# Two steps of the gathered experts moved on VectorE: the last modulation sums and the additions of the dense result to x

## The reference, cut to what matters

```python
sh1, sc1, g1, sh2, sc2, g2 = jnp.split(mod, 6, axis=-1)
...
h = rms_norm(x, norm2_g[layer]) * (1.0 + sc2) + sh2
x = x + g2 * grouped_moe(h, router_w, router_b, exp_w_gate[layer],
                         exp_w_up[layer], exp_w_down[layer])
```

```python
for e in range(N_EXPERTS):
    he = jax.nn.silu(t @ w_gate[e]) * (t @ w_up[e])
    y = y + combine[:, e:e + 1] * (he @ w_down[e]).astype(jnp.float32)
```

## Time and profile before

| | |
|---|---|
| median of three runs | 2367.88 us (2359.84 to 2372.94) |
| the profiled execution's own time | 2363.46 us |
| its span | 2361.7 us |
| mean granted clock of PE | 0.986 |
| PE busy | 2254.4 us (95%) |
| DVE busy | 1470.2 us (62%) |
| ACT busy | 1081.3 us (46%) |
| gathered experts of layer 0 | about 401 to 658 us |
| gathered experts of layer 1 | about 963 to 1195 us |

### The profile page before, as it was taken

One profiled execution on the slowest core, in us unless ns is written; L12 is line 12 of the kernel. 1 busy time (PEld: TensorE's weight loads), 2 busy tenths in 40 slices (PEclk: granted clock), 3 DMA queues, 4 the chain that ended last, 5 costly groups with the idle time before them and its releaser, 6 DMA issues.

```text
span 2361.7 us, 36488 instructions
## 1 busy us (share of the span) xinstructions
PE 2254.4 (95%) x15884; PEld 1967.8 (83%) x15884; DVE 1470.2 (62%) x1411; ACT 1081.3 (46%) x1125; POOL 69.5 (3%) x128
## 2 busy tenths in 40 slices
PE   6998999989989999999999999999999999999999
PEld 4677888767787799877789999887999899878998
DVE  5766889678855655798855554555555555545454
ACT  4344334467646433577643345334333443435332
POOL 2030010000000000000000000000000000020000
PEclk9999999899999999999999999999999999999999
DMA  9854999789842264799855552004555555433553
GB/s 344 309 181 164 318 318 322 247 289 378 321 143 89 67 238 169 251 365 368 301 171 183 186 174 86 2 4 148 192 184 191 169 179 196 161 95 107 179 192 112
DMA packets 261119, 477.81 MB, mean 202 GB/s; under 512 B 8464, under 2 KB 150896, under 8 KB 257632
## 3 DMA queue, kind: packets, MB, share of 16 engines
q1 hardware_dynamic: 251264, 431.81, 52.6%
q0 software_dynamic: 9696, 43.66, 5.5%
HBM read 473.30 MB, written 2.14 MB: 201 GB/s over the span
## 4 chain that ended last, share of the span: by engine, by line
PE 78%; DVE 8%; DMA 6%; ACT 5%; issue 2%; SPq 0%; DVEq 0%; ACTq 0%
PE psum L977 7%; PE psum L979 7%; PE psum L978 7%; PE psum L994 3%; PE psum L995 3%; PE psum L996 3%; DVE w_lo L2594 3%; PE psum L948 3%; PE psum L950 3%; PE psum L949 3%; PE psum L1361 3%; PE psum L1362 3%; PE psum L1363 3%; PE psum L1276 2%; PE psum L1278 2%; PE psum L1277 2%
## 5 line engine op out<-in xcount | busy, mean ns | idle before, releaser
L2594 DVE TENSOR_TENSOR w_lo<-ring,w_hi 128x2048 fp32r<-128x2048 f32 x320 | 730.9, 2289 | 455.0 <-ACT w_hi L1987 450.7
L1987 ACT ACTIVATE w_hi<-ring 128x2048 fp32r<-128x2048 f32 x320 | 611.5, 1914 | 543.1 <-PE psum L979 140.4
L977 PE MATMUL psum<-h_hi,w_hi 128*128 128x256 f32 x1408 | 398.9, 283 | 1.6 <-DVE h_lo L3245 1.3
L979 PE MATMUL psum<-h_hi,w_lo 128*128 128x256 f32 x1408 | 398.4, 283 | 0.0
L978 PE MATMUL psum<-h_lo,w_hi 128*128 128x256 f32 x1408 | 398.4, 283 | 0.0
L977 PEld LDWEIGHTS psum<-h_hi,w_hi 128*128 128x128 f32 x1408 | 270.1, 192 | 3.6 <-issue 1.7
L978 PEld LDWEIGHTS psum<-h_lo,w_hi 128*128 128x128 f32 x1408 | 270.1, 192 | 1.4
L979 PEld LDWEIGHTS psum<-h_hi,w_lo 128*128 128x128 f32 x1408 | 270.1, 192 | 0.0
L2594 DVE TENSOR_TENSOR w_lo<-pool,w_hi 128x2048 fp32r<-128x2048 f32 x65 | 148.8, 2290 | 49.0 <-ACT w_hi L1987 48.4
L1361 PE MATMUL psum<-w_hi,h_hi 128*128 128x512 f32 x384 | 157.4, 410 | 10.3 <-DVE w_lo L2594 10.0
L1987 ACT ACTIVATE w_hi<-pool 128x2048 fp32r<-128x2048 f32 x65 | 124.6, 1917 | 69.4 <-PE psum L1363 17.0
(11 more groups left out here) (456 smaller groups left out, 3983.2 us busy)
## 6 DMA issues: line engine op xcount, KB each, us to landing
ring<-in_exp_w_down SPq DMA_DIRECT2D x48, 1024.0 KB, 7.3
ring<-in_exp_w_gate SPq DMA_DIRECT2D x47, 1024.0 KB, 7.1
ring<-in_ffn_pre_w_in SPq DMA_DIRECT2D x44, 1024.0 KB, 5.1
ring<-in_ffn_post_w_in SPq DMA_DIRECT2D x44, 1024.0 KB, 5.1
ring<-in_exp_w_up SPq DMA_DIRECT2D x32, 1024.0 KB, 6.7
pool<-in_exp_w_up SPq DMA_DIRECT2D x32, 1024.0 KB, 8.1
ring<-in_ada_w SPq DMA_DIRECT2D x24, 1024.0 KB, 7.2
pool<-in_ada_w POOLq DMA_DIRECT2D x32, 768.0 KB, 6.1
```

Of the source, the lines that this page charges most:

```text
L977: pe.matmul(o, wh[:, k, fs], h_hi[:, k, :], start=k == 0, stop=False)
L979: m = pe.matmul(o, wl[:, k, fs], h_hi[:, k, :], start=False, stop=k == KD - 1)
L1987: act.activation(w_hi[:, (s["split"] + r) % 3, :], piece(s["pieces"][r]), ACT.Copy)\
L2594: dve.tensor_tensor(w_lo[:, slot, :], piece(s["pieces"][r]), w_hi[:, slot, :].bitcast(F32), ALU.subtract).then_inc(sem("w_lo"), 1)
```

## The change

In the loop over the gathered experts, for expert 0, part 30 of the sums no longer stands between the two up pieces' low parts but at the end of the body, and part 31 moves to the end of the body of expert 1. The two additions to x no longer stand together in the body of expert 3; the first goes to the end of expert 2's body, the second to the end of expert 3's. The loads, and the orders of PE, ACT, POOL and SP, stay as they are.

```diff
@@ -2986,20 +2986,12 @@
                 for e in range(SPARSE):
                     n = at["egate", e, 0]
                     split(n + 2)
-                    if e == 0:
-                        ada_part(4 * WIDE - 2)
                     split(n + 3)
-                    if e == 0:
-                        ada_part(4 * WIDE - 1)
                     if e == 0:
                         dve.wait_ge(sem("w_used"), U0 + at["down", WIDE - 1, 0] + 1)
                         for t in range(NT):
                             m = dve.tensor_tensor(y_slots[t], bank(2 * t, 2), grow[layer][1], ALU.mult)
                         m.then_inc(sem("wide_in"), 1)
-                    if e == 3:
-                        dve.wait_ge(sem("wide_in"), layer + 1)
-                        for t in range(NT):
-                            step(dve.tensor_tensor(x[:, t, :], x[:, t, :], y_slots[t], ALU.add))
                     if layer == 0 and e == MOD_AT + 1:
                         mod_cols(1, (0, 1), 3)
                     if e == 5:
@@ -3017,6 +3009,13 @@
                                              in1=bank(5), op0=ALU.mult, op1=ALU.mult).then_inc(sem("weighted"), 1)
                     for j in range(n + 6, at["egate", e + 1, 0] + 2 if e + 1 < SPARSE else 6 * NE):
                         split(j)
+                    if e == 0:
+                        ada_part(4 * WIDE - 2)
+                    if e == 1:
+                        ada_part(4 * WIDE - 1)
+                    if e in (2, 3):
+                        dve.wait_ge(sem("wide_in"), layer + 1)
+                        step(dve.tensor_tensor(x[:, e - 2, :], x[:, e - 2, :], y_slots[e - 2], ALU.add))
                     if e == 10:
                         scattered(0)
                         scattered(1)
```

## The result

The changed kernel takes 2371.9 us (median of 20 runs, 2364.52 to 2382.31), the kernel before 2367.56 us in as many. The ratio is 1.0023, with a 95% interval of 1.0013 to 1.0033: slower by 0.23%, about 5 us, inside the range that was given, and on the side of the forecast, which was +1.4 us. Three executions among all those behind the table further down ran far longer, for a reason that is not known (2883.11 and 11943.38 us of "part 31 only", 4447.60 us of the kernel before beside "kept busy, 8"); the ratios leave them out, and without its two "part 31 only" has a median of 2371.5 us.

The account below looks back on a forecast made before the run. PE bounds the kernel from 550 us on in layer 0 and in layer 1, the supply of pieces from 475 to 500 us. Terms +2.8 + 1.8 - 2.0 - 1.2 = +1.4 us gave 2369.3 us, range 2360 to 2377.

Parts of the forecast that it names:

- Piece 4 early, 3 of the 4 us lost at piece 5: Experts 0 and 1, layer 0: PE begins piece 4 4 us earlier; piece 5's load does not move, losing 3 us.
- Part 31 too late: Ahead of layer 0's modulation: PE waits about 4.2 us for part 31; start moves +2.8 us, ends 0 and +4.8.
- The modulation at half the clock: Layer 0's 64 modulation matmuls run at half the clock after the wait, 12.9 us against 11.13: +1.8 us.
- The additions, layer 0: Expert 3, layer 0: without the additions there, piece 21's low part comes earlier, -2.0 us; ends -2.5 and 0.
- The additions, layer 1: Layer 1: PE's wait ahead of expert 2's first down matmul goes, -1.2 us; other end 0.
- Sum: Whole kernel: +2.8 + 1.8 - 2.0 - 1.2 = +1.4 us, 2369.3 us on the median.
- The rival of the early start that carries through: Layer 0: pieces 5 to 11 come faster, modulation starts at 434.4 with part 31 done; -7.7, 2360.2 us; chance 0.15.
- The rival of the additions: Layer 0: freed time goes into load waits, part 31's wait as reckoned or longer; 2372.5 to 2374.5 us; chance 0.20.
- The rivals of the clock: Half clock at pieces 4 to 9 (2374.7 us, chance 0.10), or from piece 11 to 22 (2381.9 us, chance 0.05).
- the cold start of the clock at pieces 4 to 9: Experts 0 and 1: small gaps leave PE at half clock, modulation 8.2 us late; +6.8, 2374.7 us; chance 0.10.

Follow-up runs that it names:

- part 31 only: The change, but part 30 stays between pieces 2 and 3 as before, only part 31 moved to expert 1's end; 2372.93 us, ratio 1.0020 to the kernel before.
- kept busy, 8: The change, with 8 matmuls of 256 columns on constants put on PE into the wait for part 31; 2369.34 us, ratio 1.0011 to the kernel before.
- kept busy, 13: The change, with 13 matmuls of 256 columns on constants put on PE into the wait for part 31; 2371.78 us, ratio 1.0013 to the kernel before.
- sums-only: The change, but the additions to x stand together in expert 3 as before, only the sums moved; 2373.1 us, ratio 1.0024 to the kernel before.
- part 31 early: The change, but part 31 stands right behind part 30 at expert 0's end, ahead of piece 6; 2367.24 us, ratio 0.9991 to the kernel before.
- sums in the gap: The change, but parts 30 and 31 between low parts of pieces 4 and 5: 2362.99 us, 0.9977; with modulation behind expert 2's gate pieces too: 2360.79 us, 0.9981.
- modulation later: The change, but PE does the 64 modulation matmuls behind expert 2's two gate pieces; 2360.65 us, ratio 0.9972 to the kernel before.

## Why the prediction was right, point by point

- *Piece 4 early, 3 of the 4 us lost at piece 5*: right in the waits, 0.9 and 2.5 us on PE against forecast ones of 1 and 2.4. PE began piece 4 3.4 us earlier. I had it ready for the modulation 1.5 us earlier than before (436.9 against 438.4); it was ready no earlier, 37.0 us after the first gate matmul (41.0 less the wait) against 37.1.
- *Part 31 too late*: right, in place and size. A wait of 4.0 us was measured, 4.2 forecast; part 31 began at 440.61 and ended at 442.4, 441.1 forecast. The start moved by 3.9 us where the sum had +2.8, inside the ends of 0 and +4.8. The difference is piece 9: it had its low part at 435.4 (from 433.12) and not at 434.1, after DVE had waited 2.68 us for its high part. That lateness is there from piece 5 on, whose low part was ready at 420.85 and not at 419.6; 0.3 us of it is the later first gate matmul.
- *The modulation at half the clock*: right in kind, the term that was mis-sized. I took 64 x 0.202 = 12.9 us, against the 11.1 of one execution: +1.8. The 0.202 was a misreading: the two windows of the earlier trace rows hold 26 and 42 records, 68 for 64, since one that reaches over a window's edge is counted on both sides. Counted over longer windows it is 0.111 at the full clock ("kept busy, 13": 9 records in each us from 448 to 452) and 0.216 at half. Measured with the wait unfilled: 13.8 in the change, in the sums-only and in the part-31-only run. Without the wait the length was 11.3, 8.7, 11.1, 10.3, 9.7, 9.7 in six executions of as many kernels, 10.1 on average (in two of them at the later place); what sets it is not shown. If the kernel before has this average too, and its one profile a long form, the term is 13.8 - 10.1 = +3.7 us; against its own profile it is 13.8 - 11.3 = +2.5, and not +1.8. I should have bounded it by all 64 at the full clock as well: 64 x 0.111 = 7.1 us.
- *The additions, layer 0*: -2.0 forecast, -1.7 and -3.7 measured, each in one pair of executions. Right as far as that goes.
- *The additions, layer 1*: -1.2 forecast, -1.1 measured (215.2 to 215.4 us in every kernel that moves them, 216.4 in the two that do not; PE's idle time falls from 5.1 to 3.9 us). Right.
- *Sum*: with the measured terms, +3.9 + 3.7 - 2.7 - 1.1 = +3.8 us, where the medians say +4.3 and the ratio +5.4; with +2.5 for the modulation it is +2.6. The forecast was +1.4, so it had a quarter to a third of the loss. Both positive terms were too small, and that the time lay inside the range says little, since the range was 17 us wide.
- *The rival of the early start that carries through*: it did not happen; part 31 excluded it, as argued.
- *The rival of the additions*: that the additions give nothing back (2372.5 to 2374.5 us) is nearer to the median of 2371.9 than the forecast of 2369.3; the stages speak against it, layer 1 in every kernel, layer 0 in single executions.
- *The rivals of the clock*: the cold start of the clock at pieces 4 to 9 (whose matmuls would end at 445.6, not 445.8, by its own sum) did not show in the profile of the change: the clock stayed at 1.00 from 414 to 423.7 us, over gaps of 0.9 and 2.5 us (first row below). But it was nearer than I thought. In both "kept busy" runs, which have the same order up to there, the gap before piece 5 was 3.1 and 2.6 us, and the clock was at half behind it for some 3 us (second row: "kept busy, 13", piece 5 begins at 424.6); the same came behind gaps of 2.4 us ("part 31 early") and 2.6 us (both kernels with the sums in the gap), but not behind 2.5 us in "modulation later". So the length of the gap before a piece does not settle it in these profiles, and it never stayed low for pieces 4 to 9. The Trainium skill ("TensorE: Matmul & The Clock Gate", section "HAM oscillation — how this bites in real kernels") tells of bursts that each start cold behind waits longer than themselves. I had read it without that condition; the gaps of the change, 0.9 and 2.5 us, are shorter than a piece's 2.7. Behind the wait of 4.0 us the trace agrees with it. The clock came back behind the modulation after one piece, as before.

```profile
414.00:423.70 9.70, 6.29 (x27) 4.54 (x26) 6.43 (x5) 5.56 (x3) 0.00 (x0) 1.00 0.89 315
...
426.00:429.00 3.00, 3.00 (x8) 2.21 (x7) 3.00 (x2) 1.91 (x1) 0.00 (x0) 0.50 0.84 332
```

## What to carry to other kernels

Work that fills in beside a ring of loads is best put where its engine waits for a load anyway. Here part 31 as a late input of PE made a wait of 4 us. Both parts ahead of a low part that frees a buffer put the modulation at 40.1 us, and in a gap of 3.3 us at 35.9, where they delayed the next piece by 0.2 us. Moving something "behind" the urgent work means finding its last reader first: part 31 had one right behind piece 9, and was moved behind the low part of piece 11. And a wait of TensorE before slow small matmuls was paid twice here, once as idle time and once in the clock.

## What was not expected of the hardware

The length of the modulation's 64 records of one column each varied from 8.7 to 11.3 us in six kernels without a wait ahead of them, with the moment at which the clock fell (0.111 us a record before it, 0.216 after); why it fell when it did is not shown. After an idle wait of 4.0 to 4.4 us it was 13.8 us three times out of three; after 2.1 us of idle 12.0; with PE kept busy up to the start 8.9. And in code that is the same in both kernels, with the same idle time, PE was busy for 10 us longer in one execution than in another, with the clock at its lower level for some 22 us longer; that is twice what the change costs.
